# The first attention's last two turned blocks in the spare half of a score bank, and VectorE's combination ahead of its copy

## What is computed

```python
def diff_maps(q, k, v, lam):
    s = jnp.einsum("bhmqd,bhmkd->bhmqk", q, k, preferred_element_type=F32) * (DIFF_DH ** -0.5)
    a = jax.nn.softmax(s, axis=-1)
    w = a[:, :, 0] - lam * a[:, :, 1]
    return jnp.einsum("bhqk,bhkd->bhqd", w.astype(v.dtype), v)

def diff_out(o, subln_g, lam_init):
    o = rmsnorm(o, subln_g) * (1.0 - lam_init)
    B, H, L, VD = o.shape
    return o.transpose(0, 2, 1, 3).reshape(B, L, H * VD)
```

## Time and profile before

| | us |
|---|---|
| median of 3 executions | 3250.12 |
| lowest and highest | 3246.41, 3250.49 |
| the profiled execution | 3249.94 |
| its span | 3248.1 |

### The profile page before, as it was taken

One profiled execution on the slowest core, in us unless ns is written; L12 is line 12 of the kernel. 1 busy time (PEld: TensorE's weight loads), 2 busy tenths in 40 slices (PEclk: granted clock), 3 DMA queues, 4 the chain that ended last, 5 costly groups with the idle time before them and its releaser, 6 DMA issues.

```text
span 3248.1 us, 37697 instructions
## 1 busy us (share of the span) xinstructions
PE 3100.0 (95%) x14546; PEld 2423.2 (75%) x14546; DVE 2312.6 (71%) x3089; ACT 1304.0 (40%) x2124; POOL 800.5 (25%) x826
## 2 busy tenths in 40 slices
PE   7999998998999899999999999998899989999999
PEld 3577786667787788888877888855567877888787
DVE  6654455876646987778888666587644599989896
ACT  5431114662123433334454333376631344444443
POOL 1211101212111234321001344313544123433101
PEclk9999999999999999999999999999999999999999
DMA  6433352107645222227333345531123422222823
GB/s 225 154 139 119 135 204 81 46 1 259 208 155 175 91 91 78 85 87 283 107 127 118 104 130 176 173 128 39 40 70 123 156 79 90 85 78 78 295 88 110
DMA packets 118299, 406.86 MB, mean 125 GB/s; under 512 B 13704, under 2 KB 16328, under 8 KB 113642
## 3 DMA queue, kind: packets, MB, share of 16 engines
q1 hardware_dynamic: 65626, 200.42, 19.2%
q0 software_dynamic: 52496, 204.04, 17.7%
HBM read 321.50 MB, written 82.90 MB: 125 GB/s over the span
## 4 chain that ended last, share of the span: by engine, by line
PE 63%; DVE 8%; ACT 2%; issue 2%; POOL 1%; DMA 0%; POOLq 0%; ACTq 0%; DVEq 0%
PE PS L455 20%; PE PS L457 19%; PE PS L456 19%; PE PS L3351 2%; DVE HL L411 1%; POOL Sc L3606 1%; PE PS L3373 1%; PE PS L3390 1%; ACT HL L393 0%; ACT E L3435 0%; PE PS L3007 0%; DVE HT L1992 0%; DVE E L3530 0%; ACT Sc L3437 0%; DVE H L3658 0%
## 5 line engine op out<-in xcount | busy, mean ns | idle before, releaser
L455 PE MATMUL PS<-H,HL 128*128 128x512 f32 x1920 | 762.1, 397 | 15.2 <-DVE H L3658 7.2
L457 PE MATMUL PS<-H,HL 128*128 128x512 f32 x1920 | 752.8, 392 | 0.0
L456 PE MATMUL PS<-H,HL 128*128 128x512 f32 x1920 | 752.5, 392 | 0.0
L393 ACT ACTIVATE HL<-RAW 128x512 fp32r<-128x512 f32 (+1 forms) x429 | 312.0, 728 | 622.4 <-PE PS L457 561.4
L411 DVE TENSOR_TENSOR HL<-RAW,HL 128x512 fp32r<-128x512 f32 (+1 forms) x429 | 401.1, 935 | 146.9 <-ACT HL L393 137.4
L455 PEld LDWEIGHTS PS<-H,HL 128*128 128x128 f32 x1920 | 363.8, 189 | 105.0 <-issue 20.0
L456 PEld LDWEIGHTS PS<-H,HL 128*128 128x128 f32 x1920 | 363.9, 190 | 76.9 <-issue 2.6
L457 PEld LDWEIGHTS PS<-H,HL 128*128 128x128 f32 x1920 | 363.2, 189 | 76.8
L455 PE MATMUL PS<-HT,HL 128*128 128x512 f32 x720 | 282.6, 393 | 17.9 <-DVE rows L2314 15.8
L457 PE MATMUL PS<-HT,HL 128*128 128x512 f32 x720 | 281.5, 391 | 0.0
L456 PE MATMUL PS<-HT,HL 128*128 128x512 f32 x720 | 281.5, 391 | 0.0
(11 more groups left out here) (464 smaller groups left out, 5640.0 us busy)
## 6 DMA issues: line engine op xcount, KB each, us to landing
RAW<-in_w_up SPq DMA_DIRECT2D x100, 512.0 KB, 3.6
RAW<-in_w_down SPq DMA_DIRECT2D x82, 512.0 KB, 3.8
RAW<-in_w_proj SPq DMA_DIRECT2D x48, 512.0 KB, 3.6
scr_hid<-hidr POOLq DMA_DIRECT2D x36, 512.0 KB, 2.9
RAW<-in_w_wmodr SPq DMA_DIRECT2D x32, 512.0 KB, 4.4
HL<-in_w_dfwd POOLq DMA_DIRECT2D x16, 1024.0 KB, 6.8
HL<-in_w_dinv POOLq DMA_DIRECT2D x16, 1024.0 KB, 5.4
RAW<-in_w_wout SPq DMA_DIRECT2D x26, 512.0 KB, 4.4
```

The lines of the kernel that those rows point to most:

```text
L393: e.activation(part_slot(k, p)[0], src, ACT.Copy).then_inc(*k.high.mark(j, x))
L455: e.matmul(out, lh, rh, start=first, stop=False, skip_group_check=goes_on)
L456: e.matmul(out, lh, rl, start=False, stop=False, skip_group_check=goes_on)
L457: return e.matmul(out, ll, rh, start=False, stop=last, skip_group_check=goes_on)
```

## The change

The last two turned blocks (group 2) go to bank 2, columns 256 to 511, in place of bank 6. TensorE issues them between values 6 and 7, ahead of the scores of tile it+2 instead of behind them. ScalarE copies them between its two exponentials, ahead of the leave. VectorE combines the maps of tile it before it copies group 1 of tile it-1.

```diff
--- before.py
+++ after.py
@@ -1250,13 +1250,13 @@
                     x.then_inc(*s.pe.mark("s", j, m))
 
     def turn(j, c):
-        claim(6)
+        b, at, n = turn_at(c)
+        claim(b)
         e.wait_ge(*s.dve.at("w", j))
-        n = 4 if c < 2 else 2
         for q in range(n):
-            x = e.transpose(PS[:, 6, blk(q)], weights_of(k, j, 0)[:, blk(4 * c + q)], k.ident[:, :])
+            x = e.transpose(PS[:, b, at + 128 * q:at + 128 * q + 128], weights_of(k, j, 0)[:, blk(4 * c + q)], k.ident[:, :])
         x.then_inc(*s.pe.mark("turn", j, c))
-        free[6] = [turned1(k, j, c)]
+        free[b] = [turned1(k, j, c)]
 
     def values(j, kbs):
         if kbs[0] == 0:
@@ -1288,16 +1288,23 @@
         if 1 <= it < 33:
             turn(it - 1, 1)
         if 2 <= it < 34:
-            values(it - 2, [4, 5, 6, 7, 8, 9])
+            values(it - 2, [4, 5, 6])
+        if 1 <= it < 33:
+            turn(it - 1, 2)
+        if 2 <= it < 34:
+            values(it - 2, [7, 8, 9])
         if pair_of(it, 5) is not None:
             if it < 34:
                 free[7] = []
             rows_out(pair_of(it, 5))
         if it + 2 < 32:
             scores(it + 2)
-        if 1 <= it < 33:
-            turn(it - 1, 2)
     return free
+
+
+def turn_at(c):
+
+    return (6, 0, 4) if c < 2 else (2, 256, 2)
 
 
 def turned1(k, j, c):
@@ -1306,8 +1313,8 @@
 
 def turn_out1(k, j, c):
 
-    n = 4 if c < 2 else 2
-    return k.WT1[:, j % 2, 4 * c:4 * c + n, :], k.PS[:, 6, 0:128 * n].rearrange("p (k n) -> p k n", k=n)
+    b, at, n = turn_at(c)
+    return k.WT1[:, j % 2, 4 * c:4 * c + n, :], k.PS[:, b, at:at + 128 * n].rearrange("p (k n) -> p k n", k=n)
 
 
 def act_att1(k, e):
@@ -1423,10 +1430,10 @@
             most(it + 1, 1)
         if it < 32:
             factor(it)
+        if it < 32:
+            combine(it)
         if 1 <= it < 33:
             turn(it - 1)
-        if it < 32:
-            combine(it)
         if pair_of(it, 3) is not None:
             squares_of(pair_of(it, 3))
```

## The result

| | us |
|---|---|
| changed kernel, median of 4 executions | 3224.30 (3222.53 to 3226.22) |
| kernel before, median of 4 | 3248.26 (3241.34 to 3250.49) |
| ratio, 95% interval | 0.993, 0.9913 to 0.9947 |
| profiled execution of the changed kernel | 3223.28 |
| its span | 3221.5 |

The change makes the kernel faster by 24.0 us (3248.26 - 3224.30), 0.7%. One of ten executions of one experiment's kernel (VectorE's swap alone, e2) ran at a mean granted clock of 0.245 and took 12068 us, the nine others 3239 to 3247: it is left out of every comparison, and it happens to be that kernel's profiled one, from which only rows ahead of 900 us are used.

A forecast was written before the change was run, and what follows sets the result against it. TensorE, busy 95%, was taken as the bound, its transposes waiting on ScalarE's copy from bank 6. 28 x 0.69 = 19.4, plus 2.9 at the ends, gives 22.3 us: 3227.7 us, range 3223 to 3235.

The forecast's parts named there:

- The pass: TensorE's pass per tile falls from 6.53 to 5.84 us, or 6.05 with output blocks, gaining 0.69 each.
- The cut in the value products: Splitting the six last value products around the two transposes costs zero, at most 0.1 us a pass.
- New wait 1: TensorE's two transposes claim bank 2 from VectorE's first maximum of the tile after; covered by 0.8 us.
- New wait 2: The scores' fifth product needs bank 2 from ScalarE's copy of the two blocks; covered by 1.6 us.
- Forecast margin: VectorE's chain from maximum to copy hands over at 5.71, TensorE arrives at 5.84 or 6.05: 0.13 us, the smallest margin.
- The swap: VectorE's combination ahead of its copy of four blocks, instead of behind it; by itself costed at nothing.
- The ends: Four terms at the attention's first and last tiles: 0.9 - 0.1 + 1.2 + 0.9 = 2.9 us gained.
- The clock: One lower-clock slice near the stage's end stays, perhaps shifted; one coming or going is about 1.6 us.
- (a): Rival: VectorE's copy becomes the gate of the next tile's transposes; 3232 to 3238 us, chance 0.15.
- (b): Rival: something unseen holds the pass, leaving 0.2 us gain each; 3244 us, chance 0.04.
- (c): Slower rival: bank 2's users in a ring, scores waiting for a late ScalarE copy; 3258 us, chance 0.03.

The follow-up runs named there:

- e5: Changed kernel with the early transposes put in bank 6 instead of bank 2, and VectorE's copy ahead of its combination: 3271.09 us.
- e6: Changed kernel with ScalarE's copy of the two blocks left behind the second exponential: 3246.74 us.
- e7: Changed kernel with the two transposes behind all six last value products instead of amid them: 3225.66 us.
- e10: Changed kernel with one extra 128x512 VectorE copy a pass, between factor and combination: passes 5.92 and 6.05 us, 167.43 for the 28.
- e1: Changed kernel with VectorE's order as before, copy ahead of combination: median 3224.43 us, ratio to the kernel before 0.9936.
- e3: Changed kernel run again unaltered: median 3226.13 us against 3244.44 for the kernel before, ratio 0.9938.
- e11: Changed kernel a third time, in five rounds beside the kernel before: median 3223.57 us against 3245.83, ratio 0.9939.
- e4: Kernel before run again unaltered for its profile: profiled execution 3244.74 us.

## Why the prediction was right, and where it was off

- *The pass.* Forecast 5.84 and 6.05 us, a gain of 0.69 a pass and 19.4 in 28 (28 x 0.69 is 19.3); measured 5.84, 6.05 and 19.43. Its terms were TensorE's own steps from start to start, which didn't change, and the 0.91 with a wait in it, which became 0.21. e5 shows that the bank is needed for it, and e6 that ScalarE's order is.
- *The cut in the value products.* Taken at zero with an upper bound of 0.1 a pass; zero (e7).
- *New wait 1, two transposes on the first maximum.* The transposes come 2.51 into the pass (672.18 to 674.69) and the maximum is out at 1.60 (672.28 + 1.42 + 0.08 = 673.78; the 0.08 is its read-out): covered by 0.9, forecast 0.8.
- *New wait 2, the scores on ScalarE's copy.* The copy ends at 3.35, forecast 3.58, and the scores come to bank 2 at 5.3, forecast 5.2: covered by 2.0, forecast 1.6. What a copy at 5.74 does is e6.
- *VectorE.* Forecast margin 0.13 us, measured 0.26 by e10. The mis-sized term is the start of the maximum: the hand-over of 0.14 was taken from a row in which transposes released VectorE; behind the scores it is 0.03 (675.67 + 2.42 = 678.09, start 678.12), 0.11 less. The swap, costed at nothing, is worth nothing (e1, e2).
- *The ends.* Forecast 2.9, measured 0.73 + 2.23 = 2.96 in the first profile, but the parts were wrong and cancelled, which is luck. Tile 0: 0.9 forecast, 0.73, and in e3 and e11 a loss of 1.9 and 1.7 at the lower clock. Tile 29 to 30: -0.1 forecast, 0.0 (5.59 and 5.58). Tile 30 to 31: +1.2 forecast, +2.84 (6.45 to 3.61), as the lower-clock slice that had stretched that step is no longer there. Tile 31 to its value products: +0.9 forecast, -0.60 (4.33 to 4.93). The step that failed is that the prediction looked only at when the turned blocks would be copied; the value products also claim bank 7, whose reader is ScalarE's output copy, and the tiles now follow each other closely enough for that to be late (the idle 0.55 and 0.62 in the rows of the end). The next stage then started 0.28 later after them than before, with the clock low from 715.1 on (0.02 to 0.03 later in e3 and e11).
- *The clock.* One slice of the lower clock was expected to stay near the end of the stage; it did, only later. The Trainium skill's sentence on transposes (TensorE: Matmul & The Clock Gate, "Part 4: PE-mode transpose") would have cost another 1.6 us by the prediction's reading. The trace shows no sign of it: in the 142.72 us of the middle, where ten of the 26 products of an even pass and twelve of the 28 of an odd one are transposes, the granted clock is 1.00, and in the last three tiles, from 695.97 to 715.00, it is 1.00 as well.
- *The whole.* 22.3 forecast; 22.11 in the stage in the first profile, 19.7 and 19.9 in e3 and e11, so that the first is nearer to the forecast than the repeats. The time came out at 3224.3 against 3227.7 forecast, through the 4.5 us before and behind the stage, of which the prediction had nothing. The 24.0 us of the first comparison and the 20.5 over all executions lie on the two sides of the forecast. The rivals: (a) did not happen, and e10 shows that it would begin at 0.26; (b) did not happen; (c) was excluded by ScalarE's order, and e6 shows that it would have taken the kernel back to its old time, not 10 us beyond.

## What to carry to other kernels

Where one engine is the bound, read its steps from start to start and take a wait out by giving its cause work to run beside; the whole idle time is gained as long as each other engine's chain, walked from the same zero point, ends ahead. A spare half of a PSUM bank is good for that, but it ties the bank's users into a ring, and the order in the reader's own queue (here ScalarE's copy ahead of its second exponential) is needed as much as the new place: without it the whole gain was gone. At the ends of such a pipeline walk every buffer's claim, not only the one that was late before.

## What the runs showed of the hardware

- VectorE's maximum starts 0.14 us after the modelled end of TensorE's transposes that released it, and 0.03 after that of the scores (678.09 to 678.12 in the rows above). Whether this is the number of waits to work off or the kind of product was not tested apart.
- A VectorE copy in SBUF of 128x128 adds 0.14 us between two other instructions and one of 128x512 adds 0.34, while their own rows say 0.23 and 0.43 us: successive instructions overlap by 0.09.
- Executions of one kernel spread over 7 us (3220.6 to 3227.2, 13 of the changed kernel) and 15 us (3238.4 to 3253.3, 33 of the one before), while the 28 middle passes, at the upper clock throughout, repeat to 0.02. At least a part of the spread is where the clock falls: the stretch ahead of tile 0 has 27 us of the lower clock in the first profile of before and 20 in e4, and takes 5.1 us longer in the former.
